# The mixer's steps behind halves of a projection tile in place of thirds: 48 places in a hand-written order table in place of 72

## What is computed

```python
def mixer(h, ...):
    proj = h @ w_in                      # q|k|v, z, beta, a, and b|c|h of the short convolution
    qkv = silu(causal_dw_conv(qkv_ext, conv_gdn))
    q = l2_normalize(q) * GDN_DK ** -0.5;  k = l2_normalize(k)
    o, s = gdn_chunks(q, k, v, beta, g, s0, chunk)   # per head: gated delta rule
    o = o * rsqrt(mean(o * o) + eps) * gdn_norm * silu(z)
    y_sc = gate_b * causal_dw_conv(gate_c * h_in, conv_sc)
    return concatenate([o, y_sc]) @ w_out

def gdn_chunks(...):                     # for each chunk
    tmat = b * (k k^T) * d_strict + I    # lower triangular
    u = solve(tmat, b * v);  w = solve(tmat, b * exp(G) * k)
    nv = u - w @ s
    o = (q * exp(G)) @ s + (q k^T * d_incl) @ nv
    s = e_last * s + k_tail^T @ nv
```

## Time and profile before

| | us |
|---|---|
| median of 3 runs (1384.47 to 1385.21) | 1384.97 |
| the profiled execution | 1386.26 |
| its span | 1384.5 |
| TensorE matmul busy | 1366.1 (99%) |
| VectorE busy | 859.4 (62%) |
| ScalarE busy | 638.3 (46%) |

### The profile page before, as it was taken

How to read it: one execution, slowest core, us unless ns; L and a number is a source line. 1 busy time by engine, 2 the same in 40 slices (tenths; PEclk the granted TensorE clock), 3 DMA queues, 4 the chain that set the end, 5 groups by cost and what they waited for, 6 DMA issues and landing times.

```text
span 1384.5 us, 25009 instructions
## 1 busy us (share of the span) xinstructions
PE 1366.1 (99%) x10614; PEld 1339.5 (97%) x10614; DVE 859.4 (62%) x1527; ACT 638.3 (46%) x1025; POOL 35.8 (3%) x164
## 2 busy tenths in 40 slices
PE   9999999999999999999999999999999999999997
PEld 9999999999999999999999999999989999999997
DVE  6655533798796855543386555337977967555433
ACT  5443333593635544333354443336836355444332
POOL 0000000120000000000000000001200000000000
PEclk9999999999999999999999999999999999999998
DMA  7544344422126344434435443444222263444342
GB/s 234 205 152 152 110 142 145 153 92 96 65 93 219 119 134 146 152 114 147 162 127 202 136 150 124 146 140 139 92 99 73 88 216 122 152 152 153 126 148 99
DMA packets 50479, 190.98 MB, mean 138 GB/s; under 512 B 6368, under 2 KB 8928, under 8 KB 49856
## 3 DMA queue, kind: packets, MB, share of 16 engines
q1 hardware_dynamic: 49760, 184.26, 39.7%
q0 software_dynamic: 608, 5.12, 0.9%
HBM read 182.93 MB, written 6.43 MB: 137 GB/s over the span
## 4 chain that ended last, share of the span: by engine, by line
PE 91%; DVE 5%; ACT 3%; issue 1%; DMA 0%; SPq 0%; ACTq 0%; DVEq 0%
PE PS L1643 26%; PE PS L1645 26%; PE PS L1644 26%; PE PS L1683 2%; PE PS L1688 2%; PE PS L1684 2%; PE PS L1850 1%; DVE CV L1299 1%; DVE WL L1136 1%; PE PS L1848 1%; PE PS L1955 1%; PE PS L1974 1%; PE PS L1699 0%; DMA RAW<-in_w_up 0%; DVE PR_S L1511 0%
## 5 line engine op out<-in xcount | busy, mean ns | idle before, releaser
L1643 PE MATMUL PS<-XH,WH 128*128 128x336 f32 (+1 forms) x1728 | 550.1, 318 | 0.3 <-DVE WL L1136 0.2
L1644 PE MATMUL PS<-XL,WH 128*128 128x336 f32 (+1 forms) x1728 | 543.0, 314 | 0.3 <-issue 0.3
L1645 PE MATMUL PS<-XH,WL 128*128 128x336 f32 (+1 forms) x1728 | 543.2, 314 | 0.0
L1136 DVE TENSOR_TENSOR WL<-RAW,WH 128x1024 fp32r<-128x1024 f32 (+1 forms) x308 | 394.0, 1302 | 194.4 <-ACT WH L793 194.1
L793 ACT ACTIVATE WH<-RAW 128x1024 fp32r<-128x1024 f32 (+1 forms) x308 | 339.2, 1119 | 219.8 <-DMA RAW<-in_w_down 169.6
L1643 PEld LDWEIGHTS PS<-XH,WH 128*128 128x128 f32 x1728 | 324.9, 188 | 4.9 <-issue 3.2
L1644 PEld LDWEIGHTS PS<-XL,WH 128*128 128x128 f32 x1728 | 325.1, 188 | 0.9 <-issue 0.6
L1645 PEld LDWEIGHTS PS<-XH,WL 128*128 128x128 f32 x1728 | 324.9, 188 | 0.0
L1643 PE MATMUL PS<-HH,WH 128*128 128x336 f32 (+1 forms) x704 | 221.2, 314 | 0.0
L1645 PE MATMUL PS<-HH,WL 128*128 128x336 f32 (+1 forms) x704 | 220.5, 313 | 0.0
L1644 PE MATMUL PS<-HL,WH 128*128 128x336 f32 (+1 forms) x704 | 220.3, 313 | 0.0
(11 more groups left out here) (285 smaller groups left out, 1202.5 us busy)
## 6 DMA issues: line engine op xcount, KB each, us to landing
RAW<-in_w_up SPq DMA_DIRECT2D x172, 512.0 KB, 4.4
RAW<-in_w_down SPq DMA_DIRECT2D x64, 704.0 KB, 4.1
RAW<-in_w_in SPq DMA_DIRECT2D x56, 512.0 KB, 4.4
RAW<-in_w_out SPq DMA_DIRECT2D x16, 512.0 KB, 4.4
SEQ_S<-in_states SPq DMA_DIRECT2D x2, 2048.0 KB, 10.0
out_state_s<-SEQ_S POOLq DMA_DIRECT2D x2, 2048.0 KB, 6.9
RAW<-in_w_up SPq DMA_DIRECT2D x8, 256.0 KB, 5.6
X<-in_x SPq DMA_DIRECT2D x8, 168.0 KB, 5.0
```

Of the source, the lines that this page charges most:

```text
L1136: dve.tensor_tensor(WL[slot][:, cols], RAW[slot][:, cols], WH[slot][:, cols].bitcast(F32), ALU.subtract).then_inc(split_lo.sem, 1)
L1643: pe.matmul(out, wh, xh, start=first, stop=False)
L1644: pe.matmul(out, wh, xl, start=False, stop=False)
L1645: return pe.matmul(out, wl, xh, start=False, stop=last)
```

## The change

A tile is cut in two parts of 4 k-steps in place of three of 3, 3 and 2. The table has 24 x 2 = 48 places. What stood at the positions 3, 6 and 8 of a tile stands at 4 and 8; a few places are merged and some steps are also moved against each other. The steps themselves, the projection's matmuls and every helper are the same. In the list of the steps that use PSUM banks the order changes at three points: `y 0 2` comes ahead of `x 2 4` and `tread`; `x 2 8` ahead of `x 0 8`, `kt 2` ahead of the `y` of level 8, `x 0 16` next to its `y`; and `st 2` behind `x 1 32`, `x 1 64` behind `nv 0`.

```diff
-PARTS = 3
-PART_KT = [(0, 3), (3, 6), (6, KT)]
+PARTS = 2
+PART_KT = [(0, KT // 2), (KT // 2, KT)]
...
     [("gate_turn",)],
     [("evac", 2), ("evac", 3)],
-    [],
     [("silu", 0), ("tap", 1), ("sq", 0), ("evac", 4), ("hi", 2, 0)],
-    [],
...
-    [("evac", 12), ("unit", 1)],
-    [("x", 0, 2), ("y", 2, 2), ("silu", 9)],
-    [("lo", 5, 1), ("mirror", 2, 2), ("conv", 10), ("nt", 1), ("x", 2, 4), ("tread",)],
-    [("silu", 10), ("y", 0, 2), ("y", 2, 4), ("hi", 6, 0), ("tap", 12), ("x", 1, 2)],
-    [("hi", 6, 1), ("mirror", 0, 2), ("lo", 6, 0), ("x", 0, 4), ("y", 1, 2), ("y", 0, 4), ("hi", 7, 0), ("mirror", 1, 2)],
-    [("x", 1, 4), ("mirror", 0, 4), ("x", 0, 8), ("conv", 12), ("evac", 13)],
-    [("silu", 11), ("y", 1, 4), ("mirror", 2, 4), ("silu", 12), ("evac", 14), ("x", 2, 8), ("y", 0, 8)],
-    [("y", 2, 8), ("mirror", 2, 8), ("x", 0, 16), ("hi", 7, 1), ("lo", 6, 1), ("kt", 2), ("lo", 7, 0), ("mirror", 0, 8),
-     ("hi", 8, 0), ("mirror", 1, 4)],
+    [("evac", 12), ("unit", 1), ("x", 0, 2), ("y", 2, 2), ("silu", 9)],
+    [("lo", 5, 1), ("silu", 10), ("y", 0, 2), ("mirror", 2, 2), ("conv", 10), ("nt", 1), ("x", 2, 4), ("tread",)],
+    [("y", 2, 4), ("hi", 6, 0), ("tap", 12), ("x", 1, 2), ("hi", 6, 1), ("mirror", 0, 2), ("x", 0, 4), ("y", 1, 2),
+     ("y", 0, 4), ("hi", 7, 0), ("mirror", 1, 2)],
+    [("lo", 6, 0), ("x", 1, 4), ("mirror", 0, 4), ("x", 2, 8), ("x", 0, 8), ("conv", 12), ("evac", 13)],
+    [("silu", 11), ("y", 1, 4), ("mirror", 2, 4), ("silu", 12), ("kt", 2), ("evac", 14), ("y", 0, 8), ("y", 2, 8),
+     ("mirror", 2, 8), ("hi", 7, 1), ("lo", 6, 1), ("lo", 7, 0), ("mirror", 0, 8), ("hi", 8, 0), ("mirror", 1, 4)],
     [("tap", 14), ("hi", 8, 1), ("evac", 15)],
-    [("y", 0, 16), ("conv", 14), ("x", 1, 8)],
-    [("silu", 13), ("silu", 14), ("tap", 15)],
+    [("x", 0, 16), ("y", 0, 16), ("conv", 14), ("x", 1, 8), ("silu", 13), ("silu", 14), ("tap", 15)],
...
-    [("y", 1, 16), ("nv", 2)],
-    [("val_hi", 0), ("kt", 0), ("st", 2)],
+    [("y", 1, 16), ("nv", 2), ("val_hi", 0), ("kt", 0)],
...
-    [("hi", 10, 1), ("val_twin", 0), ("lo", 9, 1)],
-    [("yt", 0, 64), ("spread", 0, 0), ("vt", 0), ("spread", 1, 0), ("tap", 17), ("place", 1)],
+    [("hi", 10, 1), ("st", 2), ("val_twin", 0), ("lo", 9, 1), ("yt", 0, 64), ("spread", 0, 0), ("vt", 0), ("spread", 1, 0),
+     ("tap", 17), ("place", 1)],
...
-    [("ks", 0), ("x", 1, 64), ("o_cols", 2), ("val_hi", 1), ("sn", 1, 0), ("nv", 0), ("spread", 2, 0)],
-    [("conv", 17), ("o_inv", 2), ("val_lo", 1), ("lo", 10, 0), ("evac", 20), ("val_twin", 1), ("spread", 3, 0), ("o", 0),
-     ("sn", 2, 0), ("evac", 21), ("st", 0), ("conv", 19)],
+    [("ks", 0), ("o_cols", 2), ("val_hi", 1), ("sn", 1, 0), ("nv", 0), ("x", 1, 64), ("spread", 2, 0), ("conv", 17),
+     ("o_inv", 2), ("val_lo", 1), ("lo", 10, 0), ("evac", 20), ("val_twin", 1), ("spread", 3, 0), ("o", 0), ("sn", 2, 0),
+     ("evac", 21), ("st", 0), ("conv", 19)],
...
-    [("conv", 21), ("spread", 1, 1), ("sn", 0, 1), ("hi", 11, 1), ("nv", 1)],
-    [("lo", 11, 0), ("sn", 1, 1), ("o_low", 2), ("o", 1), ("spread", 2, 1), ("lo", 11, 1), ("spread", 3, 1), ("evac", 22)],
+    [("conv", 21), ("spread", 1, 1), ("sn", 0, 1), ("hi", 11, 1), ("nv", 1), ("lo", 11, 0), ("sn", 1, 1), ("o_low", 2),
+     ("o", 1), ("spread", 2, 1), ("lo", 11, 1), ("spread", 3, 1), ("evac", 22)],
```

More of the change, by code:

```diff
@@ L130 @@
     [("sq", 1), ("conv", 2), ("lo", 1, 1), ("conv", 3), ("silu", 2), ("hi", 2, 1), ("tap", 4), ("sq", 2), ("hi", 3, 0),
-     ("lo", 2, 0), ("hi", 3, 1), ("evac", 5)],
-    [("silu", 3), ("evac", 6), ("conv", 4), ("tap", 5), ("sq", 3), ("silu", 4), ("cum",), ("lo", 2, 1)],
+     ("lo", 2, 0), ("hi", 3, 1), ("evac", 5), ("silu", 3), ("evac", 6), ("conv", 4), ("tap", 5), ("sq", 3), ("silu", 4),
+     ("cum",), ("lo", 2, 1)],
     [("conv", 5)],
     [("silu", 5)],
-    [],
     [("evac", 7), ("gb", 2), ("gb", 0), ("lo", 3, 0), ("tap", 7)],
-    [],
     [("evac", 8), ("hi", 4, 0)],
@@ L140 @@
     [("qk_sum", 0), ("sq", 4)],
-    [],
     [("tap", 8), ("sq", 5), ("conv", 7), ("conv", 8), ("table",)],
-    [("qk_col", 0), ("lo", 4, 0)],
-    [("silu", 7)],
+    [("qk_col", 0), ("lo", 4, 0), ("silu", 7)],
     [("evac", 9), ("silu", 8), ("sq", 6), ("sq", 7), ("qk", 2), ("hi", 4, 1), ("qk", 0), ("qk_sum", 1), ("silu", 6),
      ("evac", 10)],
-    [("qk_col", 1), ("norms",), ("kk", 2), ("unit", 2), ("kk", 0), ("lo", 4, 1)],
-    [("nt", 2), ("qk", 1), ("unit", 0), ("hi", 5, 0)],
-    [],
@@ L150 @@
-    [("hi", 5, 1)],
-    [("nt", 0), ("x", 2, 2), ("kk", 1), ("evac", 11)],
+    [("qk_col", 1), ("norms",), ("kk", 2), ("unit", 2), ("kk", 0), ("lo", 4, 1), ("nt", 2), ("qk", 1), ("unit", 0),
+     ("hi", 5, 0)],
+    [],
+    [("hi", 5, 1), ("nt", 0), ("x", 2, 2), ("kk", 1), ("evac", 11)],
     [("lo", 5, 0), ("tap", 10)],
-    [("evac", 12), ("unit", 1)],
[4 rows of a table removed]
-    [("x", 1, 4), ("mirror", 0, 4), ("x", 0, 8), ("conv", 12), ("evac", 13)],
-    [("silu", 11), ("y", 1, 4), ("mirror", 2, 4), ("silu", 12), ("evac", 14), ("x", 2, 8), ("y", 0, 8)],
@@ L160 @@
-    [("y", 2, 8), ("mirror", 2, 8), ("x", 0, 16), ("hi", 7, 1), ("lo", 6, 1), ("kt", 2), ("lo", 7, 0), ("mirror", 0, 8),
-     ("hi", 8, 0), ("mirror", 1, 4)],
+    [("evac", 12), ("unit", 1), ("x", 0, 2), ("y", 2, 2), ("silu", 9)],
[6 rows of a table added]
     [("tap", 14), ("hi", 8, 1), ("evac", 15)],
-    [("y", 0, 16), ("conv", 14), ("x", 1, 8)],
-    [("silu", 13), ("silu", 14), ("tap", 15)],
+    [("x", 0, 16), ("y", 0, 16), ("conv", 14), ("x", 1, 8), ("silu", 13), ("silu", 14), ("tap", 15)],
     [("read",), ("key_hi", 0), ("x", 0, 32), ("conv", 15), ("evac", 16)],
-    [("lo", 7, 1)],
@@ L167 @@
-    [("silu", 15), ("key_norms",), ("mirror", 0, 16), ("place", 0), ("key_lo", 0)],
-    [],
-    [("key_twin", 0), ("y", 0, 32), ("y", 1, 8), ("mirror", 1, 8), ("lo", 8, 0), ("lo", 8, 1), ("vt", 2)],
-    [("hi", 9, 0)],
+    [("lo", 7, 1), ("silu", 15), ("key_norms",), ("mirror", 0, 16), ("place", 0), ("key_lo", 0)],
+    [],
[1 row of a table added]
     [("kst",), ("hi", 9, 1), ("key_hi", 1), ("x", 0, 64), ("x", 1, 16), ("evac", 17)],
-    [("y", 1, 16), ("nv", 2)],
-    [("val_hi", 0), ("kt", 0), ("st", 2)],
[1 row of a table added]
     [("key_lo", 1), ("evac", 18), ("oC",), ("mirror", 1, 16), ("o", 2), ("x", 1, 32), ("hi", 10, 0), ("lo", 9, 0),
@@ L184 @@
     [("kt", 1), ("yt", 1, 64)],
-    [],
     [("lo", 10, 1)],
-    [("conv", 21), ("spread", 1, 1), ("sn", 0, 1), ("hi", 11, 1), ("nv", 1)],
-    [("lo", 11, 0), ("sn", 1, 1), ("o_low", 2), ("o", 1), ("spread", 2, 1), ("lo", 11, 1), ("spread", 3, 1), ("evac", 22)],
+    [("conv", 21), ("spread", 1, 1), ("sn", 0, 1), ("hi", 11, 1), ("nv", 1), ("lo", 11, 0), ("sn", 1, 1), ("o_low", 2),
+     ("o", 1), ("spread", 2, 1), ("lo", 11, 1), ("spread", 3, 1), ("evac", 22)],
     [("rob", 0), ("o_cols", 1), ("hi", 12, 0)],
     [("evac", 23), ("tap", 23), ("sn", 2, 1)],
-    [],
     [("o_inv", 1), ("hi", 12, 1), ("lo", 12, 0), ("rob", 1)],
     [("hi", 13, 0), ("lo", 12, 1)],
-    [],
[L195 to L201, removed]
+    [("evac", 24), ("conv", 23), ("hi", 13, 1), ("o_low", 0), ("evac", 25)],
+    [("sn", 3, 1), ("o_low", 1), ("tap", 25), ("evac", 26)],
+    [],
+    [("lo", 13, 0), ("evac", 27), ("conv", 25), ("st", 1), ("finish",), ("out_o", 0), ("out_o", 1), ("out_o", 2), ("out", 0),
+     ("out", 1), ("out_o", 3), ("out", 2), ("out", 3), ("out", 4), ("out", 5), ("out", 6), ("out", 7)],
 ]
```

## The result

The changed kernel is **slower: 1390.07 us** (median of 4 runs, 1387.51 to 1392.04) against 1384.72 (4 runs, 1383.62 to 1385.21); ratio 1.0036, 95% interval 1.0025 to 1.0048. Run again on another chip beside 26 runs of before it gave 1.0030 (1.0020 to 1.0040). The forecast was 1387.5, its range reached to 1390.2, 0.1 above the result; its likeliest case, no change that can be told, did not come about. The profiled execution of the changed kernel, 1392.04, is the slowest of its four.

What follows compares the result with a forecast made beforehand. TensorE was taken as the bound. Terms of +0.57 us per layer, +1.1 in all, plus instruction supply of +0.3 and +1.1 gave +2.5: median 1384.97 to 1387.5 us, 8-in-10 range 1384.0 to 1390.2.

Steps and rivals of the forecast that it cites:

- the clock falling in layer 0: Rival: the granted clock falls in layer 0's mixer as in layer 1, price 1.7 us, total 1389.2 us; chance 0.20.
- the early waits: Up to `qk 2`: the waits of `gate_turn` and `gb` shrink, TensorE stands one position further at 306.90, -0.46 us per layer.
- price of a place: Switching between projection matmuls and small groups costs 0.16 us; six TensorE places fewer give -1.0 us per layer.
- supply, layer 0: Instruction supply at the denser bursts near position 120: 1.15 us of wait against 0.85 now, +0.3 us.
- supply, layer 1: Instruction supply at the denser bursts near position 120: 2.3 us of wait against 1.2, +1.1 us.
- clock, layer 1: Behind the supply wait near 1023 us, the fall to 1.2 GHz costs the same 1.7 us again: no change.
- `y 0 16`: Joined with `x 0 16` at 136, it waits for VectorE's evacuation of `x`: +0.6 us, between 0.4 and 1.2.
- `o 1`: Joined with `sn 0 1` and `nv 1` at 192, it waits for the evacuation of `nv`: +0.83 us, between 0.7 and 1.5.
- positions 176 and 179/180: Joining `ks 0` to `st 0` at 176 adds +0.65, but waits ahead of `ks 0` and `ks 1` go: +0.05 net.
- bursts cost no more: Rival: instruction pieces are requested early enough that denser bursts cost no more than before, 1386.1 us; chance 0.22.
- the edges miss the bursts: Rival: piece edges miss the bursts, so present supply waits and low clock go, -2.7 us, 1382.3 us; chance 0.10.
- VectorE is late in the joined places: Rival: waits of `y 0 16`, `o 1` and `o 0` reach upper bounds, 0.6 + 0.7 + 0.5 per layer, 1390.0 us; chance 0.08.

Runs made afterwards that it cites:

- Experiment 8: The kernel before with positions 174 to 224 placed as in the changed kernel, all else untouched: 1388.19 us, ratio 1.0021.
- experiment 9: Also best2: the kernel before with the changed kernel's early places, `y 0 2` ahead of `x 2 4`, `st 2` at 168, 179 moved to 180: 1382.42 us, ratio 0.9982.
- experiment 6: The changed kernel with 32 more TensorE instructions at its start, shifting the edges of the 256-instruction pieces: 1390.91 us, ratio 1.0043.
- experiment 1: The changed kernel with 168 more TensorE instructions at its start, shifting the edges of the 256-instruction pieces: 1386.61 us, ratio 1.0012.
- experiment 3: The kernel before with positions 110 to 136 alone placed as in the changed kernel: 1387.41 us, ratio 1.0018.
- experiment 4: The changed kernel with `x 0 16` back at 128 and the places 174/176 and 190/192 of before: 1386.60 us, ratio 1.0016.
- experiment 5: The changed kernel again, unchanged, on another chip, against the kernel before: 1388.64 us, ratio 1.0030.
- experiment 7: The changed kernel with positions 110 to 136 as in the kernel before: 1385.75 us, ratio 1.0012.
- experiment 11: The changed table to position 172 with `x 0 16` at 132, before's places behind it except 180, 120 more instructions at the start: 1384.02 us, ratio 0.9995.
- best3: best2 with the 64 tiny matmuls of `tread` moved from position 115 to 107: 1384.38 us, ratio 0.9993 to the kernel before.

## Why the prediction was right and wrong

The median moved by 5.1 us, from 1384.97 to 1390.07, where +2.5 was forecast. That it stayed under the range's end, 1390.2, is luck: two of the four runs lie above it, and the range's upper part stood for rivals that did not come about (the clock falling in layer 0) or came in part. The two profiled executions differ by 1392.04 - 1386.26 = 5.8 us. By the steps of the prediction:

| step | forecast | measured |
|---|---|---|
| the early waits, both layers | -0.9 | -0.9 |
| price of a place and new waits, both layers | +2.1 | +2.9 |
| supply, layer 0 | +0.3 | +0.2 |
| supply, layer 1 | +1.1 | +1.0 |
| clock, layer 1 | 0 | +2.2 |
| outside the two mixers | 0 | +0.4 |

The clock's row is layer 1's 4.24 less the others (1.1 for its places with the early waits, 0.97 for the supply). Counted by itself it comes out the same: at the low clock large matmuls start 0.28 us apart in place of 0.153; with 20 such distances after and 7 before, and the small groups among them, the difference is 2.1 to 2.2 us.

- **The early waits** were right to 0.05 us, and with the mechanism: `gate_turn` and `gb` wait less, tile 7 and `qk 2` give it back.
- **The price of a place** was smaller where nothing else changed (94 and 96: 0.01 for one place fewer, where 0.16 was taken) and larger around 120 and 128, where I had added +0.55 for new waits and two places less, +0.23 together, and -0.53 was measured. `y 2 8` did not wait.
- **The new waits inside places.** `y 0 16`: 0.6 forecast, +0.73. `o 1`: the term was +0.83; its wait grew by 0.94 (1.17 from start to start in place of 0.23). **The term that failed is that of positions 176 and 179/180**: +0.05, less 0.16 for a place, was forecast, +0.47 measured. I let `ks 1`'s wait go because a whole half stands behind `st 0`; but the join had made VectorE late by as much, so the wait stayed at 0.24 and `rob 2` got one of 0.23. Experiment 8 has these places alone, at +1.4 us a layer, and experiment 9 shows that without the join the same k-step does take both waits away. This error, +0.58 a layer, is more than made up by that at 120 and 128, -0.76; it is luck that the sum of the places came out only 0.3 too low. The late joins cost 1.0021 by themselves.
- **The supply** was right in size (1.01 and 2.19 us of loss, 1.15 and 2.3 forecast; the third wait gone) but by a rule that experiment 6 refutes: a piece is not there 3.85 us behind an edge; pieces come at least 3.3 us behind each other. Here both rules happened to give nearly the same, and in layer 0 the size is luck too: the second trace of the same kernel has 0.56 us from start to start in place of 1.17. The Trainium skill, "Runtime: NRT & Kernel Launch", section "Instruction fetch mechanics", calls the loading of instructions hidden; by the 2.02 us of idle time in this trace and by experiments 1 and 3 that rule does not hold for bursts of tiny matmuls.
- **The clock: the second term that failed, and the larger one.** I took the fall behind 1023 us for one of the same length. It grew from 3.4 us to 10.2 in both profiles of the changed kernel, which costs some 2.2 us more. The length is not a function of the wait alone (experiments 3 and 4: 6.8 us and none, after 1.92 and 1.89), and it differs from run to run, so the medians take a part of it: of the 4.2 us between the medians of experiment 5, 3.2 stand between its runs with a high mean clock and those of before, two runs only. That is what places and supply add up to in the table, 3.2. What sets the length is open.

The rivals: that bursts cost no more is refuted by the idle time in the trace and by experiment 1, and experiment 3 agrees. That the edges miss the bursts is what experiment 1 made happen. That the clock falls in layer 0 too was seen in no profile. That VectorE is late in the joined places was half true, at 176 and 180, at a third of its price.

By groups the ratios add up: positions 110 to 136 alone 1.0018 and everything else 1.0012, together 1.0030, the value of experiment 5. Each has an interval of about 0.001 either way, so this agrees and proves little. Taking the late joins' 1.0021 from the 1.0012 leaves -0.0009 for what is early and in the middle; but the shorter waits for the supply in experiment 7 are part of that.

## What to carry to other kernels

In a hand-ordered list, joining places saves little (0 to 0.36 us each here) while putting both ends of a chain through another engine into one place costs that engine's whole latency (0.7 to 0.9 us), and makes it late for the next place too. Take over the shifts that remove a wait, one by one, and leave the chains open: best2 is faster than both kernels with the same work. Where tiny matmuls follow each other by the hundred, look at the idle time by "issue" and count the instructions between two of them before making it denser; where the waits will fall, counting did not tell (experiments 6 and 11).

## What was not expected of the hardware

- Pieces of 256 TensorE instructions start to come 3.3 us or more apart in 13 traces, whatever the edges do; so the shortest way through five pieces of small groups is some 17 us, and the region from 115 to 136 is close to it.
- A wait at an edge 6.0 and 5.9 us behind the one before (experiment 1, 0.47 and 0.57 us from start to start), and one after 5.5 (experiment 11): the piece had been started only 3.1 to 3.7 us behind the edge. Why is open.
- The clock's fall came in lengths of 3.4, 6.8 and 10.2 us, after waits of 0.95 to 2.20 us from start to start, in seven traces, and not at all in four others with waits of 0.87 to 1.89 us. The seven falls begin 1017.2 us (six) or 1020.6 us (one, best3) behind the trace's first record of the full clock, which stands at 4.5 to 7.3 us, whatever the table, while the waits end 1015.6 to 1019.5 us behind it. So how a wait lies against these points may decide as much as its length; nothing here tests that. That the falls differ from run to run of the same kernel shows in the mean clocks, 0.994 to 0.997 in experiment 5; the Trainium skill, "TensorE: Matmul & The Clock Gate", Part 1, says that the number of slow matmuls is run-variable at a kernel's start, and by these mean clocks it is so in its middle too.
